# Mixer stage of a decoder layer: page ring starts with another buffer, level ahead of the turned v, scores per batch

## What is computed

```python
def decoder_layer(x, c, pos, moba_fn, gla_s0, gla_chunk, ...):
    m = ada_modulation(c, w_ada, b_ada)
    h = x * (1.0 + m[:, 1]) + m[:, 0]
    x = post_norm_residual(x, swiglu(h, w_ffn1_in, w_ffn1_out), m[:, 2], 0.5, ...)
    h = x * (1.0 + m[:, 4]) + m[:, 3]
    qm, km, vm, qg, kg, vg, gg, log_a = mixer_projections(h, pos, w_mix_in, w_gk_up, b_gk)
    o_moba = moba_fn(qm, km, vm)
    o_gla, s_fin = gla_chunked(qg, kg, vg, log_a, gla_s0, gla_chunk)
    mix = jnp.concatenate([o_moba, gla_output(o_gla, gg, ...)], axis=-1) @ w_mix_out
    x = post_norm_residual(x, mix, m[:, 5], 1.0, ...)
    h = x * (1.0 + m[:, 7]) + m[:, 6]
    x = post_norm_residual(x, swiglu(h, w_ffn2_in, w_ffn2_out), m[:, 8], 0.5, ...)
    return x, km, vm, s_fin
```

## Time and profile before

| what | value |
|---|---|
| median of three runs | 996.29 us |
| the profiled execution | 995.78 us |
| its span, first to last instruction | 993.8 us |
| TensorE busy | 916.5 us |
| VectorE (DVE) busy | 545.8 us |
| ScalarE (ACT) busy | 359.2 us |
| read from HBM | 195.0 MB |

### The profile page before, as it was taken

One profiled execution on the slowest core, in us unless ns is written; L12 is line 12 of the kernel. 1 busy time (PEld: TensorE's weight loads), 2 busy tenths in 40 slices (PEclk: granted clock), 3 DMA queues, 4 the chain that ended last, 5 costly groups with the idle time before them and its releaser, 6 DMA issues.

```text
span 993.8 us, 17303 instructions
## 1 busy us (share of the span) xinstructions
PE 916.5 (92%) x6991; PEld 797.4 (80%) x6991; DVE 545.8 (55%) x839; ACT 359.2 (36%) x509; POOL 28.0 (3%) x34
## 2 busy tenths in 40 slices
PE   6999999999999999889877999866899999999997
PEld 2588888888998699887555786646869999989994
DVE  0445444445665686665763537452666665565655
ACT  1423322233442545433641526141242323233433
POOL 0000000000000000000000000000400000000000
PEclk9999999999999999999998989896999999999999
DMA  9799888985557734256849899998414646434511
GB/s 331 246 300 260 242 234 251 254 241 146 149 149 233 242 113 129 69 178 244 286 163 373 291 331 331 323 314 254 128 43 129 168 130 168 129 103 117 149 57 53
DMA packets 214885, 199.93 MB, mean 201 GB/s; under 512 B 9569, under 2 KB 161261, under 8 KB 214678
## 3 DMA queue, kind: packets, MB, share of 16 engines
q1 hardware_dynamic: 213412, 194.99, 63.4%
q0 software_dynamic: 704, 2.49, 0.8%
q10 hardware_dynamic: 690, 1.35, 0.4%
HBM read 195.00 MB, written 3.80 MB: 200 GB/s over the span
## 4 chain that ended last, share of the span: by engine, by line
PE 80%; DVE 9%; ACT 4%; DMA 3%; issue 3%; SPq 2%; ACTq 0%; DVEq 0%
PE B L691 19%; PE B L692 18%; PE B L696 18%; PE B L751 4%; PE B L887 3%; PE B L898 2%; PE B L936 2%; PE B L760 2%; PE B L791 2%; SPq L619 2%; DMA ring<-in_cache_v 1%; PE B L775 1%; PE B L1017 1%; ACT kT L1240 1%; PE B L717 1%
## 5 line engine op out<-in xcount | busy, mean ns | idle before, releaser
L691 PE MATMUL B<-Hh,wh 128*128 128x320 f32 x912 | 275.7, 316 | 0.6 <-issue 0.6
L692 PE MATMUL B<-Hl,wh 128*128 128x320 f32 x912 | 271.8, 311 | 0.0
L1595 DVE TENSOR_TENSOR wl<-raw,wh 128x2048 fp32r<-128x2048 f32 x90 | 207.3, 2305 | 93.5 <-ACT wh L1240 86.6
L1240 ACT ACTIVATE wh<-raw 128x2048 fp32r<-128x2048 f32 x90 | 172.2, 1913 | 149.5 <-PE B L696 115.0
L691 PEld LDWEIGHTS B<-Hh,wh 128*128 128x128 f32 x912 | 173.7, 190 | 11.0 <-issue 10.2
L692 PEld LDWEIGHTS B<-Hl,wh 128*128 128x128 f32 x912 | 173.6, 190 | 0.3
L696 PE MATMUL B<-Hh,wl 128*128 128x320 f32 x912 | 152.3, 309 | 0.0
L696 PEld LDWEIGHTS B<-Hh,wl 128*128 128x128 f32 x912 | 138.4, 188 | 0.0
L691 PE MATMUL B<-Gh,wh 128*128 128x320 f32 x352 | 106.0, 314 | 2.5 <-DVE Gl L1721 2.5
L692 PE MATMUL B<-Gl,wh 128*128 128x320 f32 x352 | 105.8, 314 | 0.0
L1240 ACT ACTIVATE sg<-B 128x320 f32<-128x320 f32 x46 | 20.1, 437 | 207.3 <-PE B L696 193.8
(11 more groups left out here) (246 smaller groups left out, 945.7 us busy)
## 6 DMA issues: line engine op xcount, KB each, us to landing
raw<-in_w_ffn_in SPq DMA_DIRECT2D x88, 512.0 KB, 6.2
raw<-in_w_ada SPq DMA_DIRECT2D x72, 512.0 KB, 5.0
ring<-in_cache_k SPq DMA_DIRECT2D x108, 256.0 KB, 4.9
ring<-in_cache_v SPq DMA_DIRECT2D x84, 256.0 KB, 4.9
raw<-in_w_ffn_out SPq DMA_DIRECT2D x32, 384.0 KB, 3.5
raw<-in_w_mix_in SPq DMA_DIRECT2D x24, 512.0 KB, 4.8
raw<-in_w_ffn_out SPq DMA_DIRECT2D x32, 320.0 KB, 4.1
M<-in_cache_v SPq DMA_DIRECT2D x16, 256.0 KB, 4.8
```

What stands on the lines that cost most here:

```text
L691: pe.matmul(out, w, xh[k], start=start and k == 0, stop=False)
L692: pe.matmul(out, w, xl[k], start=False, stop=False)
L1240: return act.activation(out, in_, func, **kw)
L1595: dve.tensor_tensor(wl[:, wbuf(n), :], raw_view(n), f32(wh[:, wbuf(n), :]), ALU.subtract).then_inc(lo_ready, 1)
```

## The change

The first page group goes to the ring buffer (MI + 0) % 4 = 2, then 3, 0, 1, where it was 0, 1, 2, 3. In gaps 8 and 10 the level comes ahead of the turned v (in GAPS and in `gap`; ACT and DVE keep their own orders). In `scores` each batch waits for the copies of its own keys and signals s_out by itself; the copies of the next block wait for the batch that they overwrite, the others count two signals for a block.

```diff
@@ -147,10 +147,10 @@
 GAPS[5] = [("nk", t) for t in range(3)]
-GAPS[8] = [("nv", t) for t in range(3)]
-GAPS[10] = [("nvg", t) for t in range(3)]
 for _lv in range(6):
     GAPS[6 + _lv] += mix_fills(7 + _lv)
+GAPS[8] += [("nv", t) for t in range(3)]
+GAPS[10] += [("nvg", t) for t in range(3)]
@@ -190,7 +190,7 @@
-    queue, last, buf, before = list(IN_RING) + [IN_H], {}, [], []
+    queue, last, buf, before = [(MI + x) % R for x in range(R)] + [IN_H], {}, [], []
@@ -889,15 +889,15 @@
             def scores(i, j):
 
-                wait_act(("k", i, j, 1, 3))
-                wait_dve(("k", i, j, 1, 3))
                 if 4 * i + j >= 2:
                     pe.wait_ge(s_act, 4 * i + j - 1)
                 for bi in range(2):
+                    wait_act(("k", i, j, bi, 3))
+                    wait_dve(("k", i, j, bi, 3))
                     for c in range(HP):
                         m = pe.matmul(B[j % 2][32 * c:32 * c + 32, :], Qz[:, 2 * i + bi, c, :], kT[:, bi, c, :],
                                       start=(bi == 0), stop=(bi == 1))
-                m.then_inc(s_out, 1)
+                    m.then_inc(s_out, 1)
@@ -1126,14 +1126,14 @@
+                if n >= 6:
+                    level(n - 6)
                 if n == 8:
                     pe.wait_ge(out_read, READ["MI"] + 8)
                     turn_back("nv", CV)
                 if n == 10:
                     pe.wait_ge(out_read, READ["MI"] + 10)
                     turn_back("nvg", CVG)
-                if n >= 6:
-                    level(n - 6)
@@ -1331,7 +1331,7 @@
-                            act.wait_ge(s_out, 4 * i + j)
+                            act.wait_ge(s_out, 2 * (4 * i + j) - 1 + bi)
@@ -1540,7 +1540,7 @@
-                    act.wait_ge(s_out, 4 * NPAIR)
+                    act.wait_ge(s_out, 8 * NPAIR)
@@ -1781,13 +1781,13 @@
-                            dve.wait_ge(s_out, 4 * i + j)
+                            dve.wait_ge(s_out, 2 * (4 * i + j) - 1 + bi)
             def block_values(i, j):
 
-                dve.wait_ge(s_out, 4 * i + j + 1)
+                dve.wait_ge(s_out, 2 * (4 * i + j) + 2)
```

## The result

| | before | after |
|---|---|---|
| median, us | 997.16 | 982.72 (979.93 to 983.45) |
| profiled execution, us | 995.78 | 983.45 |
| its span, us | 993.8 | 981.3 |

A forecast was written before the change was run, and what follows sets the result against it. TensorE, busy for 92% of the span, was taken as the bound, so gains must come from its idle or slow time. 10.3 + 0 + 5.0 = 15.3 us less gave 981.0 us, range 978.0 to 988.0 for 8 in 10.

The forecast's parts named there:

- Part 1: Projection, gaps 8 and 10: the level ahead of the turned v saves 10.3 us, bounds 6.8 and 10.3.
- its own walk: Projection, new order followed with durations of before: last slot ends at 444.0, formerly near 454.2; gain given as 10.3 us.
- the second way of counting: Projection: the level's two waits, 6.83 us, plus 3.2 us lost at the lower clock after them, in all 10.0.
- the rival of another wait in gaps 8 and 10: Projection: a 9.0 us circle outlasts the 8.2 us of slot and level; total 984.3, or 989 without scores' gain; chance 0.12.
- Part 2: Page ring beginning with buffer 2: first page issued near 405 us instead of 428.77, worth 0, bounds 0 and 1 us.
- the cover of 10 us: End of key stage: MO+2's load, issued later, still lands 10 us before ACT takes it, so cost 0.
- Part 3: Key stage, scores and copies per batch: the scores' waits for kT are covered, 5.0 us less, bounds 0 and 5.3.
- All six lie on the chain, with DVE or TensorE work next: Key stage: the six waits of scores for kT all count toward the time, giving the 5.0 us.
- more than counted: Rival: DVE-paced stretches between 462 and 510 us shorten, or TensorE keeps full clock more; 3 us more, 978; chance 0.10.
- The pages: Rival, key stage: waits for v pages take back the scores' gain; total 986.0, or 983.5 with half; chance 0.20.
- the slower rival: Key stage: small pauses lower TensorE's clock, scores take 2.97 us for 1.92, total 1002.8; chance 0.04.
- The sum: Whole kernel: 10.3 + 0 + 5.0 = 15.3 us less, time given as 981.0 us.

The follow-up runs named there:

- the kernel with copies first: Kernel before, TensorE's order unchanged, ACT emptying the turned v's banks ahead of its rounding (slot 8) and sigmoids (slot 10): 987.85 us for 997.62, ratio 0.9916.
- the one kept busy: Kernel before with 4 and 3 useless matmuls put behind the turned v in gaps 8 and 10: 997.27 us for 997.62, ratio 0.9992.
- the kernel without the ring: Changed kernel with the page ring's start put back as before, the level order and per-batch scores kept: 983.0 us, ratio 0.9841 to the kernel before.
- The ring alone: Kernel before with only the page ring beginning at buffer 2: 994.23 us, ratio 0.9975.
- the two traces of the changed kernel: The changed kernel, nothing altered, measured and traced twice: 982.72 us, ratio 0.9848, then 983.06 us for 998.32, ratio 0.9834.
- part 3 alone: Kernel before with only the scores and key copies waiting and signalling per batch: 989.96 us, ratio 0.9934.

## Why the prediction was right, point by point

**Part 1: right in place, mechanism and size.** Forecast 10.3 (by its own walk, 454.2 less 444.0, it is 10.2), and 10.1 came in the stretch, in every trace of a kernel with this part. The idle waits were 6.8 of it and the clock the rest, as the second way of counting had it: the kernel with copies first shows the bank as the cause, the one kept busy the clock's share with the waits not shortened (3.1, of which 2.5 remained). The 0.8 us of slack that I gave each level was enough, and the rival of another wait in gaps 8 and 10 has no row in any trace.

**Part 2: right.** 0 forecast, and the kernel without the ring has the same pieces up to the third L950 with its first page 18 us later. The ring alone measured 0.9975, which its trace does not tie to pages. By the Trainium skill's rule ("DMA: Bandwidth & Descriptors", "Rules for kernel authors") it should have paid; here no gain is measured with it, and no row of before shows an instruction that waits for that data. The tail came as told: MO+2 is issued 3.7 us ahead of the last L950 (668.31), where it was 10.7 ahead before (671.46, with L950 at 682.1), so 7.0 later, and the cover of 10 us held:

```profile
664.59 3.58 SPq L569 DMA_DIRECT2D raw<-in_w_mix_out  x4
668.21 17.41 SPq L587 DMA_DIRECT2D raw<-in_w_ffn_in  x6
```

**Part 3: right in mechanism, one step wrong, mis-sized in both directions.** The sum had 5.0. The pair of traces gives 4.7 for the key stage, but before's trace has the shortest key stage of its kind. Five traces with whole scores give 226.2 to 229.6 (mean 228.3), six with halves and otherwise equal copies 221.2 to 223.0 (mean 222.0): 6.4 us, and the two groups don't meet. What the halves did at once is as counted: the six scores end 1.06, 0.81, 0.81, 0.82, 0.81 and 0.81 us sooner after the transposes ahead of them, 5.1 in all. Four of them in the trace of after:

```profile
450.39 2.19 PE L898 MATMUL B<-kT,Qz 128*32 128x512 f32 x16
...
472.85 2.01 PE L898 MATMUL B<-kT,Qz 128*32 128x512 f32 x16
...
530.23 2.01 PE L898 MATMUL B<-kT,Qz 128*32 128x512 f32 x16
...
543.18 1.94 PE L898 MATMUL B<-kT,Qz 128*32 128x512 f32 x16
```

The step that failed is "All six lie on the chain, with DVE or TensorE work next". The scores at 543.18 do not: the work next behind them waits for DVE, whatever the scores do. Behind them TensorE comes to L1011 sooner and stands there 1.11 us, where it stood 0.30 (before first, then after):

```profile
561.16 0.46 PE L1011 MATMUL B<-W 128*128 128x128 f32 x2 [0.30 <-issue]
```

```profile
548.24 0.46 PE L1011 MATMUL B<-W 128*128 128x128 f32 x2 [1.11 <-issue]
```

It is 0.30 in all five traces with whole scores and about 1.1 in all seven with halves and before's share of the copies. The row names no engine. I take it that TensorE waits there for DVE, whose copies of keys (3.68 us for six) and of PT stand in line:

```profile
540.23 3.68 DVE L1785 COPY kT<-B 128x512 f32<-128x512 f32 x6
...
547.35 1.28 DVE L1841 COPY PT<-B 128x512 f32<-128x512 f32 x2
```

Moving one such copy to ACT made it 0.34 again, which is the evidence. So 0.8 of the 5.0 was given back at once.

What came on top (6.4 against 5.1 less 0.8) I had as the rival "more than counted". Keys to values gave 2.6 where two covered waits make 1.9. Rows of before and after lead through it. The third transpose group to the next scores takes 1.5 us longer after, at the lower clock (486.69 to 492.75, for 497.72 to 502.25). The wait for PT, which DVE sets, takes 1.1 of that back, 2.53 for 3.60. Then the matmuls up to the first values need 1.9 us at full clock for 3.1 (L966, `turn_prompt`, shows the two clocks: 0.87 us for 1.54):

```profile
486.69 2.31 PE L887 MATMUL B<-cst,ring 128*128 128x128 f32 x12 [1.76 <-DVE kT L1785]
...
499.21 0.43 PE L975 MATMUL B<-Z,W 128*64 128x128 f32 x2 [2.53 <-DVE PT L1841]
...
500.29 0.87 PE L966 MATMUL B<-cst,Z 128*128 128x128 f32 x6
```

```profile
497.72 1.85 PE L887 MATMUL B<-cst,ring 128*128 128x128 f32 x12 [1.76 <-DVE kT L1785]
...
509.79 0.43 PE L975 MATMUL B<-Z,W 128*64 128x128 f32 x2 [3.60 <-DVE PT L1841]
...
511.39 1.54 PE L966 MATMUL B<-cst,Z 128*128 128x128 f32 x6
```

1.9 - 1.5 + 1.1 + 1.2 = 2.7: a stretch at the lower clock lay where DVE sets the pace after, and in front of the value matmuls before. From L1011 to the third L950 the length goes with the clock among the kernels with whole scores: 89.4 us in before and with the ring alone, at a mean granted clock of 0.90, and 92.2 to 92.6 in the three others, at 0.87. The halves did not bring more full clock as such: over the key stage it is 0.88 to 0.91 in those six, 0.89 to 0.91 in the five with whole scores. What differs is where the slow stretches lie; that this makes the rest of the 6.4 is argued from the rows above, not shown by an edit. Why the clock falls where it does in one order and not in another stays open.

**The rivals.** The pages took nothing back: 14.3 and 14.4 us of waits in the two traces of the changed kernel, 15.5 with part 3 alone, 16.0 before. (Part 3 alone has the longer wait for key pages told above.) Nor did many small pauses bring the clock down in the scores: the rows above have 1.94 to 2.19 us, where the slower rival wanted 2.97 in ten or more. Two of the sixteen are slow in after (3.01 and 3.23), the same two as in before (2.97 and 3.28). By the Trainium skill ("TensorE: Matmul & The Clock Gate", "A second HAM failure mode: psum-queue depth-cycling"), which describes a bf16 kernel whose clock goes up and down with short idle times between groups of matmuls, it would have been the outcome; no trace here shows it.

**The sum.** 10.1 and 4.7 stand in the two traces, against 10.3 and 5.0. The stretches behind the last values and the stages ahead took 2.3 of it in this pair, where the sum had nothing; and none of the three edits changes work there. The medians' difference is 14.4. That 981.0 lies 1.7 us from 982.72 is in part luck: in part 3 the step that was wrong (0.8 us too much) and what came on top (2.1 too little) went against each other, and these 2.3 us against the rest.

## What to carry to other kernels

When an engine waits for a buffer, look at who empties it and what stands ahead of that in its queue; moving the consumer's work to a free buffer, or the emptying ahead of a long job, returns the wait and also what ran at the lower clock behind it. Issuing a transfer earlier gained nothing that shows here, where no instruction waited for it; look for that row first. Of several waits of one line, check each for what comes next behind it: one of these six had another engine's work behind it, which took its 0.8 us back, and only an edit on that engine brought it out.

## What the hardware showed that I had not expected

Where the granted clock falls was repeated in the two traces of the changed kernel, and moves with small edits; behind the norm's mean and ahead of `level(1)` it differs between kernels that are alike there, so it isn't fixed by the order of work alone. From L1011 to the third L950 the time at the lower clock (twice one minus the mean granted clock, times the length, since the levels are 2.4 and 1.2 GHz) is 17.9 us in before and with the ring alone, 24.0 in the three other kernels with whole scores, 19.7 in the six with part 1, halves and before's share of the copies, 14.1 with part 3 alone (the clock has two digits, so each within 0.9 us). The ring edit, which touches no matmul, changed keys to values from 57.0 to 59.9 us, at a granted clock of 0.92 for 0.98.

What lies ahead of `level(1)` varies by 5 us between traces (it starts at 404.4 to 409.3) in kernels that are alike there, more than some of the effects looked for. Comparing stretches between fixed instructions is what made 0.8 us readable.

Inside a run of value matmuls TensorE pauses for 0.6 to 1.9 us where the code has no wait; the row of after, with no engine named:

```profile
653.65 0.30 PE L941 MATMUL B<-vnew,arow 128*32 128x128 f32 x1 [1.66 <-issue]
```

A like pause stands in every trace; its cause was not tried.
